# Seven block products for eight in the down projection of a hybrid decoder step

## The chip, the cores and the metric

The kernel runs on one core of one Trainium2 chip, in one launch. The core has a matrix engine (TensorE, PE in the profile), VectorE (DVE), ScalarE (ACT), GpSimd (POOL) and SyncE (SP), whose queue issues most transfers here. The metric is the time on the device in microseconds (us). Three runs of the kernel before took 1352.70, 1354.54 and 1359.77 us, median 1354.54.

## The reference, cut to what matters

A prompt of 1024 positions and 8 sample rows (1032 columns together) pass a layer: RMSNorm, a wide input projection, four groups of heads, an output projection with a residual add, and then the feed-forward part, which is what the change touches:

```
D_MODEL = 1024; D_FF = 2816; CONV_W = 3
def conv_ffn(x, g, w_up, conv_w, conv_b, w_down, buf):
    t = x.shape[1]
    up = rmsnorm(x, g) @ w_up
    ext = jnp.concatenate([buf.astype(up.dtype), up], axis=1)
    conv = conv_b + sum(ext[:, i:i + t] * conv_w[i] for i in range(CONV_W))
    a, gate = jnp.split(conv, 2, axis=-1)
    y = (jax.nn.silu(gate) * a) @ w_down
    return y, ext[:, t:]
...
        xp = xp + f.astype(xp.dtype)
```

The down projection is the product with `w_down` (2816 x 1024) and the residual add behind it. All is float32.

## The kernel before, in words

Everything is transposed: features lie on the 128 partitions, positions in the columns. A float32 product is made of three products of reduced-precision parts (`f32r`): each operand x is split into high = round(x) on ScalarE (an `ACTIVATE` with Copy) and low = x - high on VectorE (a `TENSOR_TENSOR`), and TensorE adds hi*hi + hi*lo + lo*hi in PSUM. So every tile of an operand costs one pass on ScalarE and one on VectorE before TensorE can take it.

The **up projection** runs over 22 pairs of tiles (`FT = 22`, index p or c). Each p is already seven block products P1 to P7 (a Strassen-Winograd scheme over half-blocks), each of 24 matmuls of 258 columns (`HC = 258`; two chunks make half of the 1032 columns, 516). Convolution, silu and the gate product follow on VectorE and ScalarE, and SP stores the resulting activation tile `va` to `scr_act[p]` in DRAM (`act_store`, L848).

The **down projection** before goes over eight output tiles d, 22 contraction tiles f and three column chunks of 344. Its activations are loaded back from `scr_act` (L864), split once, and kept in SBUF in all 22 tiles (`fh`, `fl`). The weights come in 24 groups (`GRAN`): a load (`down_load`, L857), a high split (`down_hi`, L1900), a low split (`down_low`, L2750), with two buffers in turn. The matmuls are L1410 to L1412. The first four groups serve d = 0 and 1 together; then one output tile after the other is finished, `add_y` (L2824) adds its PSUM banks to the residual loaded by GpSimd (L2938), and GpSimd stores it (L2933). Tiles d alternate between two sets of three banks, so the next tile's matmuls go on while one is evicted. The last tile is finished by chunk (L2835) and stored by SP (L900).

What sets the order is the code alone: each engine runs its own list, written out by hand, and waits on counting semaphores. `p_done` counts finished products or groups of TensorE (`NPROD` of them before the down projection), `st_hi` and `st_lo` the weight splits, `mv_hi` and `mv_lo` the activation splits, `x2_add` the evictions, `act_st` the stores of activations. An engine that waits holds all that stands behind it in its list; SP's list of loads too.

Of the kernel before, what the change touches and what calls it, by code (L numbers as in the profile page):

```python
# [18 lines left out]
P = 128  # L19
# [12 lines left out]
CH = 344  # L32
# [66 lines left out]
def build(nc, t):  # L99
# [5 lines left out]
    with ctx:  # L105
# [161 lines left out]
        fh = []  # L267
        for n, o5 in ((0, Q), (1, Q + 8256), (2, set0), (3, set0 + 8256), (4, Q + 16512), (5, Q + 24768), (6, Q + 33024),
                      (7, Q + 41280), (12, set1), (13, set1 + 8256), (14, set1 + 16512), (19, conv0), (20, conv0 + 8256),
                      (21, base)):  # L270
            h_, o6 = at(f"fh{n}", [P, COLS], f32r, o5)
            fh.append((n, h_[:, :], at(f"fl{n}", [P, COLS], f32r, o6)[0][:, :], at(f"fr{n}", [P, COLS], f32, o6)[0][:, :]))
        fh = {n: (h_, l_, r_) for n, h_, l_, r_ in fh}
        for j in range(KC):
            fh[8 + j if j < 4 else 11 + j] = (hhi[:, j, :], hlo[:, j, :], hlr[:, j, :])
        dst2 = [spare, set0 + 16512]
        dnh, dnl, dnr = [], [], []
        for n in range(2):
            h_, o6 = at(f"dnh{n}", [P, 1024], f32r, dst2[n])
            dnh.append(h_)  # L280
            dnl.append(at(f"dnl{n}", [P, 1024], f32r, o6)[0])
            dnr.append(at(f"dnr{n}", [P, 1024], f32, o6)[0])
        yst = at("yst", [P, COLS], f32, base + 8256)[0]
# [191 lines left out]
        NG = len(GRAN)  # L475
        g_end = {d: max(n for n in range(NG) if d in GRAN[n][0]) for d in range(KC)}
# [81 lines left out]
        def _(sp):  # L558
# [291 lines left out]
            def down_load(n):  # L850
                dd, fa_, fb_ = GRAN[n]
                w = len(dd) * P
                if n >= 2:
                    sp.wait_ge(S("p_done"), NPROD + n - 1)
                src = dnL[fa_:fb_, :, dd[0] * P:dd[0] * P + w].rearrange("f p c -> p f c")
                dst = dnr[n % 2][:, 0:(fb_ - fa_) * w].rearrange("p (f c) -> p f c", c=w)
                sp.dma_start(dst, src).then_inc(S(f"wgt_ld{n % 2}"), 16)  # L857
            def act_loads(done, p, fs):
                sp.wait_ge(S("p_done"), p_no[done, p])
                for f in fs:  # L860
                    sp.wait_ge(S("act_st"), 16 * (f + 1))
                    if f >= 4:
                        sp.wait_ge(S(f"stage_ld{f % 4}"), 16 * (12 + f // 4))
                    sp.dma_start(fh[f][2], scr_act[f]).then_inc(S(f"stage_ld{f % 4}"), 16)  # L864
            for c in range(FT):
# [23 lines left out]
            sp.wait_ge(S("act_st"), 16 * FT)
            act_loads("P3", FT - 1, (19, 20))  # L890
# [6 lines left out]
            for ch in range(3):
                sp.wait_ge(S("x2_add"), 2 * KC + ch)
                cs = slice(ch * CH, (ch + 1) * CH)
                sp.dma_start(t["o_yT"][:, KC - 1, cs], yst[:, cs]).then_inc(S("out"), 16)  # L900
            sp.wait_ge(S("out"), 16 * (3 + 3))
            sp.wait_ge(S("y_out"), 16 * (KC - 1))
# [51 lines left out]
        def _(pe):  # L954
# [446 lines left out]
            def down(n, d, f, chs, first, last):  # L1401

                dd, fa_, fb_ = GRAN[n]
                w = len(dd) * P
                c = (f - fa_) * w + (d - dd[0]) * P
                hi_, lo_ = dnh[n % 2][:, c:c + P], dnl[n % 2][:, c:c + P]
                a_hi, a_lo, _ = fh[f]
                for ch in chs:
                    out, cs = ps[:, 3 * (d % 2) + ch, 0:CH], slice(ch * CH, (ch + 1) * CH)
# [26 lines left out]
        def _(act):  # L1436
# [465 lines left out]
            for c in range(FT):  # L1902
                more = c + 1 < FT
                if c:
# [11 lines left out]
                    if more:  # L1916
                        w_vec(c + 1)
# [1082 lines left out]
```

## Time and profile before

| | |
|---|---|
| Median of the runs shown | 1354.54 us (1352.70 to 1359.77) |
| Profiled execution: span | 1348.4 us |
| Its own time beside the span | not recorded; the median of the runs is 6.1 us more than its span |
| TensorE busy | 1302.1 us, 97% of the span |
| VectorE, ScalarE, GpSimd busy | 946.2, 555.1 and 217.1 us |
| Moved by DMA | 206.82 MB, mean 153 GB/s |
| Down projection, first matmul to the end | 1092.79 to 1345.4 us |

The page gives busy time by engine, then the chain of work that ended last, followed back from the last instruction. Matmuls overlap: each shows about 0.28 or 0.32 us of its own while one starts every 0.12 or 0.16 us, so the pace is read from starts, and a wait from the idle time in square brackets. Between 700 and 1060 us the profile is periodic (18 pairs p); from 1132 us on it is periodic by output tile.

### The profile page before, as it was taken

To read this page: it belongs to the slowest core of one execution; us is meant where nothing else is said; L and a number is where in the kernel's file an instruction comes from. 1 tells how busy PE (TensorE), PEld (TensorE's weight loads), DVE (VectorE), ACT (ScalarE), POOL (GpSimd) and SP (SyncE) were. 2 spreads that over 40 slices of the span, in tenths; PEclk is the share of its full clock that TensorE was granted. 3 is DMA by queue.
4 is the path that set the end of the run, shared out by engine and by line. 5 is a ranking of instruction groups with operands and counts; after the bars stand their busy time and mean duration, and the time that the engine had idled before them with its cause. 6 is when DMAs were issued, how large, how long until landed. Compare 5 with 4: busy or idle time off the path is not lost.

```text
span 1348.4 us, 24281 instructions
## 1 busy us (share of the span) xinstructions
PE 1302.1 (97%) x9271; PEld 1198.1 (89%) x9271; DVE 946.2 (70%) x1390; ACT 555.1 (41%) x913; POOL 217.1 (16%) x222
## 2 busy tenths in 40 slices
PE   7999999989989999999999999999999999999999
PEld 5888787767667678899999999999999998999999
DVE  6678889988898767567697888887788894211111
ACT  6623111355567665343545435445445463000100
POOL 0420034323333430100201101101101000000000
PEclk9999999979999999999999999999999999999999
DMA  9868766679999772421322222222222383322222
GB/s 304 302 208 252 208 176 182 211 225 259 295 322 354 227 224 76 148 97 62 94 88 70 96 71 71 95 71 71 96 71 71 124 302 115 106 85 81 75 75 75
DMA packets 151071, 206.82 MB, mean 153 GB/s; under 512 B 12862, under 2 KB 112728, under 8 KB 150676
## 3 DMA queue, kind: packets, MB, share of 16 engines
q1 hardware_dynamic: 133204, 146.74, 35.0%
q0 software_dynamic: 12848, 46.73, 10.9%
q10 hardware_dynamic: 4904, 11.81, 2.9%
q8 instruction: 73, 1.20, 0.4%
q14 instruction: 42, 0.34, 0.1%
HBM read 174.91 MB, written 29.82 MB: 152 GB/s over the span
## 4 chain that ended last, share of the span: by engine, by line
PE 74%; DVE 10%; DMA 5%; issue 3%; POOL 3%; SPq 3%; ACT 1%; ACTq 0%; DVEq 0%; POOLq 0%
PE ps L1349 9%; PE ps L1350 9%; PE ps L1351 9%; PE ps L1410 6%; PE ps L1411 6%; PE ps L1412 6%; PE ps L1191 4%; PE ps L1132 3%; PE ps L1134 3%; PE ps L1133 3%; PE ps L1214 2%; PE ps L1290 1%; DMA upr<-in_w_upL 1%; PE ps L1292 1%; PE ps L1291 1%
## 5 line engine op out<-in xcount | busy, mean ns | idle before, releaser
L1349 PE MATMUL ps<-hhi,uph 128*128 128x258 f32 x704 | 200.8, 285 | 1.3 <-ACT ug L1828 0.7
L1350 PE MATMUL ps<-hlo,uph 128*128 128x258 f32 x704 | 199.5, 283 | 0.0
L1351 PE MATMUL ps<-hhi,upl 128*128 128x258 f32 x704 | 199.2, 283 | 0.0
L2750 DVE TENSOR_TENSOR dnl<-dnr,dnh 128x896 fp32r<-128x896 f32 (+2 forms) x24 | 27.2, 1135 | 176.3 <-ACT dnh L1900 176.3
L1349 PEld LDWEIGHTS ps<-hhi,uph 128*128 128x128 f32 x704 | 133.9, 190 | 2.6 <-DVE ug L2708 1.4
L1350 PEld LDWEIGHTS ps<-hlo,uph 128*128 128x128 f32 x704 | 134.1, 190 | 0.0
L1351 PEld LDWEIGHTS ps<-hhi,upl 128*128 128x128 f32 x704 | 133.6, 190 | 0.0
L1132 PE MATMUL ps<-whi,hhi 128*128 128x512 f32 (+1 forms) x336 | 125.7, 374 | 0.9 <-PE ps L1134 0.6
L1134 PE MATMUL ps<-whi,hlo 128*128 128x512 f32 (+1 forms) x336 | 124.4, 370 | 0.0
L1133 PE MATMUL ps<-wlo,hhi 128*128 128x512 f32 (+1 forms) x336 | 124.0, 369 | 0.0
L1410 PE MATMUL ps<-fh,dnh 128*128 128x344 f32 x336 | 107.5, 320 | 3.2 <-DVE dnl L2750 3.2
L1411 PE MATMUL ps<-fl,dnh 128*128 128x344 f32 x336 | 107.8, 321 | 0.0
L1412 PE MATMUL ps<-fh,dnl 128*128 128x344 f32 x336 | 107.2, 319 | 0.0
L1900 ACT ACTIVATE dnh<-dnr 128x896 fp32r<-128x896 f32 (+2 forms) x24 | 23.7, 987 | 194.7 <-DMA dnr<-in_w_down 194.7
L2925 POOL TENSOR_TENSOR upr<-upr 128x512 f32<-128x512 f32 x22 | 30.8, 1398 | 447.0 <-DMA upr<-in_w_upL 447.0
L1191 PEld LDWEIGHTS ps<-vst,pts 128*128 128x128 f32 x576 | 72.3, 198 | 30.4 <-issue 27.4
L1769 ACT ACTIVATE uph<-upr 128x1024 fp32r<-128x1024 f32 (+1 forms) x66 | 79.3, 1202 | 39.6 <-DMA upr<-in_w_upL 36.1
L2628 DVE TENSOR_TENSOR upl<-upr,uph 128x1024 fp32r<-128x1024 f32 (+1 forms) x66 | 92.1, 1396 | 0.1
L1191 PE MATMUL ps<-vst,pts 128*128 128x65 f32 x576 | 79.5, 285 | 9.1 <-DVE oN L2333 7.1
L2862 POOL DMA_INDIRECT vring<-in_cache_a_v,gtab x64 | 62.3, 973 | 137.0 <-PE ps L1214 130.8
L2020 DVE TENSOR_TENSOR ring<-ring,qb 128x1024 f32<-128x1024 f32 x64 | 78.0, 1218 | 7.3 <-DMA ring<-in_cache_a_k 5.7
L2028 DVE TENSOR_REDUCE sA<-ring 128x16 f32<-128x1024 f32 x64 | 78.0, 1219 | 1.9
(357 smaller groups left out, 3567.2 us busy)
## 6 DMA issues: line engine op xcount, KB each, us to landing
upr<-in_w_upL SPq DMA_DIRECT2D x88, 256.0 KB, 3.3
ring<-in_cache_a_k SPq DMA_DIRECT2D x170, 128.0 KB
scr_act<-va SPq DMA_DIRECT2D x22, 516.0 KB, 2.6
ring<-in_cache_a_k ACTq DMA_DIRECT2D x86, 128.0 KB
wst<-in_w_in SPq DMA_DIRECT2D x32, 256.0 KB, 3.9
fr<-scr_act SPq DMA_DIRECT2D x14, 516.0 KB, 5.2
dnr<-in_w_down SPq DMA_DIRECT2D x12, 448.0 KB, 4.2
dnr<-in_w_down SPq DMA_DIRECT2D x10, 512.0 KB, 4.0
```

The source lines that it names most:

```text
L1132: pe.matmul(out, lh, whi[:, sl, 0:w], start=(kc == 0), stop=False)
L1133: pe.matmul(out, lh, wlo[:, sl, 0:w], start=False, stop=False)
L1134: i = pe.matmul(out, ll, whi[:, sl, 0:w], start=False, stop=(kc == KC - 1))
L1191: i = pe.matmul(ps[:, 6, 0:HD + 1], pts[:, g % 2, j, :], vst[:, hp % 2, j, VCOL[H % 2]], start=(j == 0), stop=(j == nb - 1))
L1349: pe.matmul(out, hi_, r_hi[:, cs], start=(first and i == 0), stop=False, skip_group_check=not first)
L1350: pe.matmul(out, hi_, r_lo[:, cs], start=False, stop=False, skip_group_check=not first)
L1351: m = pe.matmul(out, lo_, r_hi[:, cs], start=False, stop=(i == 3), skip_group_check=not first)
L1410: pe.matmul(out, hi_, a_hi[:, cs], start=first, stop=False)
L1411: pe.matmul(out, hi_, a_lo[:, cs], start=False, stop=False)
L1412: m = pe.matmul(out, lo_, a_hi[:, cs], start=False, stop=last)
L1769: act.activation(uph[p % 2][:, a:b, :], upr[p % 2][:, a:b, :], ACT.Copy).then_inc(S("st_hi"), 1)
L2628: dve.tensor_tensor(upl[p % 2][:, a:b, :], upr[p % 2][:, a:b, :], uph[p % 2][:, a:b, :].bitcast(f32), ALU.subtract).then_inc(S("st_lo"), 1)
```

## The change

The down projection becomes a Strassen-Winograd scheme too. The output has two halves by feature (mi: 4 tiles each) and two by position (ni: 516 columns each), the contraction two halves of 11 tiles (`HK = 11`). With A the weight, B the activations, blocks A11 to A22 and B11 to B22:

- S3 = A11 - A21, S2 = A21 + A22 - A11, S1 = A21 + A22, S4 = A12 - S2; T3 = B22 - B12, T2 = B11 + T3, T4 = B21 - T2, T1 = B22 - T2 (the names are the code's; S2 and T4 stand there with a sign)
- P1 = A11 B11, P2 = A12 B21, P6 = S2 T2, P7 = S3 T3, P4 = A22 T4, P5 = S1 T1, P3 = S4 B22
- in PSUM: P1, then P2 on top of it gives output block 11; P6 alone, P7 on top, P4 on top; P5 alone, P3 on top. P1 is copied to SBUF (`u_p1`) before P2 goes on top, and added to three quarters of the residual by GpSimd.

The order of products is `PHASE`, 11 steps each, 77 steps in all (`NSTEP`). A step is one contraction tile: 516 columns of activations, 512 of weights, four output tiles by two chunks by three terms, 24 matmuls of 258 columns, over all eight banks. So a product fills all banks, and the next one may write bank pair j only when it is copied or evicted (`bank_free`). Operands are no longer split once and kept: every step splits its own into a ring of four slots (`bh`, `bl`, `wh`, `wl`; raw weights in `wr`), a slot is free when TensorE has finished the step four before. Raw activations stay in SBUF (`act_t`) and GpSimd forms the T sums in place; VectorE forms the S sums (`w_sum`), GpSimd S1. Weights are loaded as single tiles of 256 KB by `ring_load`, `wa_load` and `wb_load`; the residual comes in four quarters of 1.06 MB (`x_quarter`), and SP stores the output (`y_store`).

```diff
-        GRAN = [((0, 1), f, f + 4) for f in (0, 4, 8, 12)] + [((d,), 16, FT) for d in (0, 1)] \
-            + [((d,), a, b) for d in range(2, KC) for a, b in ((0, 8), (8, 15), (15, FT))]
+        PHASE = ["P1", "P2", "P6", "P7", "P4", "P5", "P3"]
+        NSTEP = len(PHASE) * HK
...
+            def ring_load(st):
...
+                sp.wait_ge(S("p_done"), NPROD + st - 3)
+                sp.dma_start(wr[st % 4][:, :], down_w(mi, HK + k)).then_inc(S(f"ring_ld{n % 4}"), 16)
...
+            for st in range(HK, NSTEP):
+                ph, k = PHASE[st // HK], st % HK
+                if st in RING_NO:
+                    ring_load(st)
+                if ph == "P2":
+                    if k == 1:
+                        x_quarter(1, xq1, 0, 1)
+                    if k == 3:
+                        x_quarter(2, xq2, 1, 1)
+                    wb_load(k)
+                if st == step_of("P6", 3):
+                    for j in range(4):
+                        y_store("P2", j)
+                if st == step_of("P6", 6):
+                    sp.wait_ge(S("y_out"), 16 * 4)
+                    x_quarter(3, xq0, 1, 0)
...
+            def bank_free(ph, j):
+                if ph == "P1":
+                    pe.wait_ge(S("c_sum"), 5 * (FT - 1) + (-1, 1, 3, 4)[j])
+                    return
+                if ph == "P2":
+                    pe.wait_ge(S("copied"), 3 * FT + j + 1)
+                    return
+                pe.wait_ge(S("x2_add"), KC + 4 * (PHASE.index(ph) - 2) + j + 1)
+            for st in range(NSTEP):
+                ph, k = PHASE[st // HK], st % HK
+                n = st % 4
+                pe.wait_ge(S("mv_lo"), MV0 + st + 1)
+                pe.wait_ge(S("st_lo"), ST0 + st + 1)
+                fresh = ph in FRESH
+                for j in range(4):
+                    if k == 0:
+                        bank_free(ph, j)
+                    hi_, lo_ = wh[n][:, j * P:(j + 1) * P], wl[n][:, j * P:(j + 1) * P]
+                    for ch in range(2):
+                        out, cs = ps[:, 2 * bank_of[j] + ch, 0:HC], slice(ch * HC, (ch + 1) * HC)
+                        pe.matmul(out, hi_, bh[n][:, cs], start=(fresh and k == 0), stop=False, skip_group_check=not fresh)
+                        pe.matmul(out, hi_, bl[n][:, cs], start=False, stop=False, skip_group_check=not fresh)
+                        m = pe.matmul(out, lo_, bh[n][:, cs], start=False, stop=(k == HK - 1), skip_group_check=not fresh)
...
+            for st in range(4, NSTEP):
+                b_hi(st)
+                w_hi(st)
+                if st == HK + 2:
+                    for j in range(4):
+                        p1_copy(j)
...
+            for st in range(4, NSTEP):
+                if st + 1 < NSTEP and PHASE[(st + 1) // HK] != "P2":
+                    w_sum(st + 1)
+                b_lo(st)
+                w_lo(st)
+                if PHASE[st // HK] == "P2":
+                    w_sum(st)
+                ph = PHASE[(st - 3) // HK]
+                if (st - 3) % HK == HK - 1 and ph in EVICT:
+                    for j in range(4):
+                        evict(ph, j)
...
+            for k in range(HK):
+                n = RING_NO[step_of("P4", k)]
+                pool.wait_ge(S(f"ring_ld{n % 4}"), ring_total(n))
+                pool.wait_ge(S("s_vec"), VEC_NO["S3", k])
+                summed(w_b[k][:, :], w_b[k][:, :], wr[step_of("P4", k) % 4][:, :], ALU.add)
```

`w_sum` waits for `ring_ld` of its step in P6, P4 and P3 and does nothing for P7 and P5; in P2 it forms S3 behind the splits. `b_hi(st)` waits until step st - 4 is finished, `evict` for its bank pair (`pair_done`, or `p_done` for the last).

Three places of the new order follow. First VectorE, where P2 ends and P6 begins: step 24 is the third of P6 (its slot is `wr_208`), `wr_213` is step 25's raw weight, `xq_225` the quarter of the residual that takes P2's banks.

```order
L2914 TENSOR_TENSOR wr_208<-wr_208,wa_185 128x512 [waits s_vec,ring_ld0]
L2894 TENSOR_TENSOR bl_221<-act_162,bh_220 128x516 [waits mv_hi]
L2902 TENSOR_TENSOR wl_224<-wr_223,wh_222 128x512 [waits st_hi]
L2914 TENSOR_TENSOR wr_213<-wr_213,wa_186 128x512 [waits s_vec,ring_ld1]
L2894 TENSOR_TENSOR bl_206<-act_163,bh_205 128x516 [waits mv_hi]
L2902 TENSOR_TENSOR wl_209<-wr_208,wh_207 128x512 [waits st_hi]
L2943 TENSOR_TENSOR xq_225<-ps,xq_225 128x516 [waits y_ld,pair_done]
L2943 TENSOR_TENSOR xq_225<-ps,xq_225 128x516 [waits pair_done] x2
L2943 TENSOR_TENSOR xq_225<-ps,xq_225 128x516 [waits p_done]
```

The four evictions of P2 (L2943) stand behind step 25's weight sum and the splits of step 24. In the kernel before, an eviction was one instruction of 1032 columns behind a weight split, and TensorE was by then on the other set of banks:

```order
L2750 TENSOR_TENSOR dnl_204<-dnr_205,dnh_203 128x1024 [waits st_hi]
L2824 TENSOR_TENSOR yst<-ps,yst 128x1032 [waits y_ld,p_done]
L2750 TENSOR_TENSOR dnl_207<-dnr_208,dnh_206 128x896 [waits st_hi]
L2824 TENSOR_TENSOR yst<-ps,yst 128x1032 [waits y_ld,p_done]
L2750 TENSOR_TENSOR dnl_204<-dnr_205,dnh_203 128x896 [waits st_hi]
```

ScalarE, where P1 ends and P2 begins: `wr_213` is step 13's weight, `u_p_228` the copy of P1.

```order
L2043 ACTIVATE wh_222<-wr_223 128x512 [waits ring_ld3]
L2032 ACTIVATE bh_205<-act_173 128x516 [waits stage_ld0,p_done]
L2043 ACTIVATE wh_207<-wr_208 128x512 [waits ring_ld0]
L2032 ACTIVATE bh_210<-act_174 128x516 [waits stage_ld1,p_done]
L2043 ACTIVATE wh_212<-wr_213 128x512 [waits ring_ld1]
L2048 ACTIVATE u_p_228<-ps 128x516 [waits pair_done] x3
L2048 ACTIVATE u_p_228<-ps 128x516 [waits p_done]
```

The copies stand behind the high split of a weight that has to be loaded first. SP's list at the same place, from the last two halves of activations on (`act_171`, `act_182`); `wr_213` is again step 13's weight:

```order
L934 DMA act_171<-scr_act 128x516 [waits x_ld0]
L934 DMA act_182<-scr_act 128x516 [waits act_st,x_ld1]
L954 DMA wr_223<-in_w_down 128x512 [waits p_done]
L947 DMA wb_194<-in_w_down 128x512
L954 DMA wr_208<-in_w_down 128x512 [waits p_done]
L959 DMA xq_226<-scr_x 128x4x516 [waits y_ld]
L947 DMA wb_195<-in_w_down 128x512
L954 DMA wr_213<-in_w_down 128x512 [waits p_done]
```

The ring's first weight loads stand behind all 40 loads of activations; between them stand two loads of A21 and one quarter of the residual. In the kernel before, all weight loads from the fifth on had SP to themselves.

## Rows read from the trace of the kernel before

**Rows 1.** The page: busy time by engine, and the chain that ended last.

```profile
PE 1302.1 (97%) x9271; PEld 1198.1 (89%) x9271; DVE 946.2 (70%) x1390; ACT 555.1 (41%) x913; POOL 217.1 (16%) x222
...
PE 74%; DVE 10%; DMA 5%; issue 3%; POOL 3%; SPq 3%; ACT 1%; ACTq 0%; DVEq 0%; POOLq 0%
```

**Rows 2.** Windows: busy us (instructions) by engine, granted clock, DMA share, GB/s.

```profile
700.00:1060.00 360.00, 359.37 (x2981) 358.43 (x2981) 295.29 (x320) 159.98 (x231) 46.99 (x36) 1.00 0.25 80
...
1132.00:1340.00 208.00, 208.00 (x1325) 208.00 (x1324) 38.18 (x35) 23.90 (x25) 7.48 (x14) 1.00 0.26 80
```

**Rows 3.** Timeline at the seams: start, us, engine, line, shapes, [idle before].

```profile
1092.79 0.32 PE L1410 MATMUL ps<-fh,dnh 128*128 128x344 f32 x1
...
1126.63 0.32 PE L1412 MATMUL ps<-hhi,dnl 128*128 128x344 f32 x1
1130.19 0.43 PE L1410 MATMUL ps<-fh,dnh 128*128 128x344 f32 x1 [3.24 <-DVE dnl L2750]
...
1345.26 0.32 PE L1412 MATMUL ps<-fh,dnl 128*128 128x344 f32 x1
...
1345.62 0.52 DVE L2835 TENSOR_TENSOR yst<-ps,yst 128x344 f32<-128x344 f32 x1 [2.78 <-PE ps L1412]
```

**Rows 4.** The chain that ended last, around the 3.24 us gap.

```profile
1128.91 1.24 DVE dnl L2750
1130.15 0.04 issue
```

**Rows 5.** Windows where the clock fell, rose and stayed; timeline at one fall.

```profile
278.00:279.00 1.00, 0.65 (x5) 0.68 (x6) 0.97 (x2) 0.98 (x2) 0.73 (x1) 0.87 1.07 369
...
285.00:286.00 1.00, 1.00 (x7) 0.85 (x6) 0.69 (x1) 0.28 (x1) 0.00 (x0) 0.71 1.18 310
...
288.00:289.00 1.00, 0.48 (x5) 0.51 (x5) 0.93 (x6) 0.00 (x0) 0.00 (x0) 0.99 0.44 143
...
295.00:296.00 1.00, 1.00 (x9) 0.83 (x12) 0.91 (x3) 0.22 (x2) 0.00 (x0) 0.59 0.42 139
...
456.00:457.00 1.00, 1.00 (x5) 0.98 (x6) 0.69 (x4) 0.80 (x4) 0.08 (x1) 0.62 0.89 274
...
459.00:460.00 1.00, 1.00 (x16) 0.17 (x8) 0.83 (x2) 0.13 (x1) 0.17 (x1) 0.68 0.56 229
...
534.00:535.00 1.00, 0.00 (x0) 0.00 (x0) 0.96 (x3) 0.61 (x3) 0.02 (x1) 0.87 0.00 0
...
541.00:542.00 1.00, 1.00 (x8) 1.00 (x8) 1.00 (x1) 0.00 (x0) 0.00 (x0) 0.72 1.02 405
...
1128.00:1129.00 1.00, 0.00 (x0) 0.00 (x0) 0.09 (x1) 1.00 (x2) 0.00 (x0) 1.00 0.71 179
...
535.63 0.55 PE L1300 MATMUL ps<-hhi,wohi 128*128 128x256 f32 x1 [2.25 <-DVE hlo L2440]
```

**Rows 6.** Landing of 256 KB loads: L568 (2 KB rows), then L813 (512 B).

```profile
DMA to landing us min/median/max: 2.0/3.9/8.2
...
DMA to landing us min/median/max: 2.9/3.1/4.4
```

**Rows 7.** Timeline: an eviction-like DVE pass, a copy, a GpSimd sum.

```profile
1086.26 0.60 ACT L1828 ACTIVATE ug<-ps 128x516 f32<-128x516 f32 x1 [4.24 <-PE ps L1351]
...
1087.28 0.69 DVE L2708 TENSOR_TENSOR ug<-ps,ug 128x516 f32<-128x516 f32 x1
1088.00 0.69 DVE L2714 SCALAR_TENSOR_TENSOR ug<-ug,rstd_bc 128x516 f32<-128x516 f32 x1
...
1056.96 1.31 POOL L2925 TENSOR_TENSOR upr<-upr 128x512 f32<-128x512 f32 x1 [18.24 <-DMA upr<-in_w_upL]
```

**Rows 8.** SP's last activation store; then windows around the seam.

```profile
1105.81 0.38 SPq L848 DMA_DIRECT2D scr_act<-va  x1
...
1090.00:1100.00 10.00, 10.00 (x71) 10.00 (x70) 8.72 (x11) 6.84 (x11) 0.00 (x0) 1.00 1.00 388
1100.00:1110.00 10.00, 10.00 (x66) 10.00 (x65) 9.96 (x10) 6.08 (x7) 0.00 (x0) 1.00 0.80 272
```

More of the change, by code:

```diff
@@ L273, in build @@
[L273 to L283, printed above, removed]
+        HK = FT // 2
@@ new lines, in build @@
+        RING_NO = {}
+        for ph_ in ("P1", "P2", "P6", "P4", "P3"):
+            for k_ in range(HK):
+                RING_NO[step_of(ph_, k_)] = len(RING_NO)
+        POOL_NO = {}
+        for name_ in ("T3", "T2"):
+            for k_ in range(HK):
+                POOL_NO[name_, k_] = 2 * FT + 2 * k_ + (1 if name_ == "T3" else 2)
+        for name_ in ("x12", "x22"):
+            POOL_NO[name_] = 2 * FT + 2 * HK + (1 if name_ == "x12" else 2)
+        for k_ in range(HK):
+            POOL_NO["T4", k_] = POOL_NO["x22"] + k_ + 1
@@ L858, in act_loads, with act_load @@
[L858 to L864, printed above, removed]
+            def act_load(f, full=False):
+                sp.wait_ge(S("act_st"), 16 * (f + 1))
+                if f >= 4:
+                    sp.wait_ge(S(f"stage_ld{f % 4}"), act_total(f - 4))
+                c = slice(0, COLS if full else H2)
+                sp.dma_start(act_t[f][:, c], scr_act[f, :, c]).then_inc(S(f"stage_ld{f % 4}"), 16)
@@ new lines, in _ @@
+                    for f in range(4):
+                        act_load(f, True)
+                    sp.wait_ge(S("p_done"), p_no["P5", FT - 1])
+                    for k in range(8):
+                        wa_load(k)
+            sp.wait_ge(S("p_done"), p_no["P2", FT - 1])
+            for f in range(4, 8):
+                act_load(f)
+            sp.wait_ge(S("p_done"), p_no["P7", FT - 1])
+            for f in range(8, 16):
+                act_load(f)
+            sp.wait_ge(S("p_done"), p_no["P3", FT - 1])
@@ L897, in _ @@
[L897 to L902, printed above, removed]
+            for f in H2_ORDER[0:8]:
+                act_load2(f)
+            sp.wait_ge(S("act_st"), 16 * FT)
+            act_load(21)
+            for f in H2_ORDER[8:]:
+                act_load2(f)
@@ L1399, in _ @@
                 seven("P3", p, slotY[p], S4_, B22, False)
[L1401 to L1409, printed above, removed]
-                    pe.matmul(out, hi_, a_hi[:, cs], start=first, stop=False)
-                    pe.matmul(out, hi_, a_lo[:, cs], start=False, stop=False)
-                    m = pe.matmul(out, lo_, a_hi[:, cs], start=False, stop=last)
-                return m
@@ L1917, in _ @@
                         w_vec(c + 1)
+                    else:
+                        w_hi(0)
+                        w_hi(1)
                     silu(c - 1)
+                    if not more:
+                        b_hi(2)
+                        w_hi(2)
                     u3_copy(c)
```

361 lines of the change are left out of this document (236 added, 125 removed).

## The prediction, made before the changed kernel ran

> **What bounds the kernel now.** I read the page first. TensorE is busy for 97% of the span and carries 74% of the chain that ended last [rows 1]. The change touches the down projection alone, so the second view is two stretches of steady matmuls, one of the up projection (258 columns) and one of the down projection (344) [rows 2]: in both TensorE is never idle for more than a fraction of a microsecond, VectorE is 82% busy in the first and 18% in the second. The third is TensorE's timeline at the seams [rows 3]: the down projection starts at 1092.79, loses one gap of 3.24 us at 1126.95, and its last matmul starts at 1345.26. So the stage is 252.6 us of TensorE, bound by the array's own pace, and everything else hides behind it. After it come one eviction of 0.52 us and one store.
>
> **The work.** Before: 8 output tiles x 22 contraction tiles x 3 column chunks x 3 terms = 1584 matmuls. The first 216 (three groups of 72) take 34.0 us up to the gap, 0.1574 us each; all of them are 249.3 us, and 252.6 - 249.3 = 3.3 us is the gap. After: 77 steps x 4 output tiles x 2 chunks x 3 terms = 1848 matmuls of 258 columns. That shape runs before the seam: 2981 in 360 us, 0.1208 us each [rows 2], so 223.2 us, and 2.90 us for one step of 24. The block products alone give -26.1 us, one eighth of the columns back and a fixed piece per matmul lost on 264 more matmuls. The old gap waited for a weight load that stood behind a store and an output on SP; that order goes, -3.3. Without any wait of its own the new stage is 29.4 us shorter.
>
> **What feeds it.** The operands are no longer split once and kept: each step splits 516 activation columns and 512 weight columns on ScalarE (0.6 each, as the copy) and VectorE (0.69 each, as the two evictions) [rows 7], at most 2.1 us of VectorE per step with a weight sum, against 2.90. GpSimd's 22+11+11 sums of 516 columns and 11 of 512 take 1.3 us each [rows 7], three adds of 2064 columns perhaps 5.2 each: 88 us over 223. T3 and T2 are wanted a whole product later. None of these is the bound by its sum. What counts is order, in three kinds of place.
>
> **a) The eviction behind the next load (P2 to P6, P7 to P4, P5 to P3).** A weight slot is refilled when the step four before is finished. VectorE's row has, ahead of the four evictions of a product, the weight sum of the *next* step, whose load SP asks for only when the product's last step is finished (the order rows of the change). TensorE's next product may not write a bank until it is evicted. So at the product's end everything runs in line: tail of the last matmul and wake-up 0.2 (a 344-column matmul lasts 0.32 at a pace of 0.157; 0.04 from VectorE's end to TensorE's start [rows 4]), landing of 256 KB, wake-up 0.1, then sum, two splits and the first eviction, 4 x 0.67 = 2.7 us. Lone loads of 256 KB landed in 3.1 us (median, pieces of 512 B) and the fastest one with 2 KB rows in 2.0 [rows 6]; I take the middle, 2.6. Gap: 0.2 + 2.6 + 0.1 + 2.7 = 5.6 us, bounds 5.0 and 6.1. Three: +16.8 us (15.0 to 18.3). The later evictions cost 0.69 against 0.72 us of matmuls per tile, so only the first is paid. Where P7 follows P6 and P5 follows P4 no load stands ahead; the splits end some 2.0 us after a step, the eviction 0.7 later, still inside a step.
>
> On that landing the Trainium skill ("DMA: Bandwidth & Descriptors", section "Anatomy of one DMA") gives 2.0 us fixed and the bytes at 436 GB/s: an estimate of 2.6 us for 256 KB, inside the two rows. That fit is for transfers issued by GpSimd; no row here shows a lone SP load with 2 KB rows.
>
> **b) P1 to P2.** ScalarE copies P1's banks out behind the high split of step 13's weight. SP reaches that load late. Its last store of activations was asked for at 1105.8 [rows 8]; VectorE now does less ahead of it, so about 1103. Behind it stand u10 (0.4 MB), 18 second halves and one first (5.0 MB), with the store 5.9 MB. At 330 GB/s, between 272 and 388 of the rows [rows 8], that is 18 us; the first weight load of the ring is asked for near 1120. Ahead of step 13's load lie then 0.8 MB of halves, four weight tiles (1.0 MB) and a quarter of x2 (1.06 MB): with its own 0.26, 3.2 MB, 9.6 us, so it lands near 1129.3. Split and first copy, 1.2: P2 starts at 1130.5. P1 ends at 1092.8 + 11 x 2.90 = 1124.7. Gap: 5.8; I take 5.5 us, 2.5 at 388 GB/s, 10 at 272.
>
> **c) The ring inside P6, P4 and P3.** A step's splits stand behind the next step's sum, so they end 0.2 + landing + 0.1 + 3 x 0.67 after the step three before; they are due two steps (5.8 us) after it. With 2.6 that is 4.9: 0.9 us to spare. It holds, but a 1 MB quarter and twice four stores pass in P6 to P5: +0.5.
>
> **d) The clock.** The granted clock fell from 2.4 to 1.2 GHz four times before the up projection [rows 5]. From the levels, the low stretches are 278.74-285.58, 288.98-295.82, 456.24-459.64 and 534.74-541.56, the last with TensorE idle until 535.63. Half of the busy time in them is lost: 3.4, 3.4, 1.7 and 3.0, mean 2.9 us. The last followed 2.25 us of idleness [rows 5], among the attention's short matmuls. Against that stands one 3.24 us gap between full-length matmuls, after which the clock was still whole (1128-1129). The new gaps are 5 to 6 us, so nearer to full idleness than any of them. I count the three of a) as falling: +8.7, bounds 0 and 4 x 3.4 = 13.6.
>
> The Trainium skill ("TensorE: Matmul & The Clock Gate", section "HAM oscillation — how this bites in real kernels") tells of a kernel that waits for a transfer at each tile and starts each next tile at the low clock. By that rule all four gaps fall, +11.6 instead of +8.7; by the 3.24 us row none need to. The four falls side with the page.
>
> **Sum.** -29.4 + 16.8 + 5.5 + 0.5 + 8.7 = +2.1 us. The profiled span is 1348.4 us; it has no own time beside it, the median of the runs shown is 1354.5, 6.1 more, which I leave as it is. Forecast 1356.6 us. Its bounds: -29.4 + 15.0 + 2.5 = -11.9 (1342.6) to -29.4 + 18.3 + 10 + 4.4 + 13.6 = +16.9 (1371.4), where 4.4 is the price of the slow ring below.
>
> **Rivals.**
> *The clock stays.* Full-length matmuls before and after each gap, as at 1127: the sum without d), -6.6 us, 1347.9. For it that one row, against it that the new gap is nearly twice as long.
> *No gaps: the change does what its work says.* The ring's load is early enough, or evictions overlap: -29.4 and some 2 for the seams, 1327. Against it is VectorE's order, which is fixed.
> *Transfers bind (slower).* The place is the ring in P6, P4, P3; it decides from a landing of 3.5 us on, where 0.2 + L + 0.1 + 2.0 passes 5.8. With all queues loaded the 256 KB loads had a median of 3.9 [rows 6]. Then a step takes (6.2 + 2.9)/3 = 3.03 us, 33 x 0.13 = +4.4; each gap a) is 1.3 longer, +3.9; b) is 10, +4.5: 1356.6 + 12.8 = 1369.4. For it: 1 MB quarters and stores on the same queue. Against it: a step moves 0.26 MB in 2.90 us, 90 GB/s, and the queues did 388.
>
> **Chances.** Forecast 0.48, spread 1350 to 1363; clock stays 0.17; no gaps 0.07; transfers bind 0.28. About 0.5% (6.8 us) is what a measurement of this kernel tells from no change: faster means under 1347.8, slower over 1361.3. Faster: all of the second rival, half of the first (0.09), 0.03 of the forecast, 0.19. Slower: most of the third (0.22) and 0.07 of the forecast, 0.29. Same 0.52. Range: from a clock that stays with quick landings, 1344, to the third rival, 1369.
>
> **What will show it.** TensorE with 1848 matmuls at 0.121 us and four idle spells: the first ended by ScalarE's copy, the other three by VectorE's eviction, each 5 to 6 us, with the weight load issued right at the product's end. The granted clock near 0.5 for 3 to 7 us behind them. No gap at P6 to P7 and P4 to P5 above 0.5 us. Waits at single steps inside P6, P4 or P3 would speak for the third rival. I am wrong if the three gaps are absent or under 3 us, if the copy of P1 comes in time, or if matmuls of 258 columns run slower with this operand pattern than in the up projection.

## The result

The changed kernel took 1388.47 us (median of 4 runs, 1386.09 to 1389.79) against 1353.62 us of the kernel before beside it (4 runs, 1347.31 to 1359.77): ratio 1.0257, 95% interval 1.0218 to 1.0296. It is 2.6% slower; 1356.6 us was forecast, and the forecast's range ended at 1369.

The two profiled executions have spans of 1348.4 and 1386.2 us, +37.8. First the page of the changed kernel, beside [rows 1]: busy time by engine, and the chain that ended last.

```profile
PE 1287.6 (93%) x9535; PEld 1180.7 (85%) x9535; DVE 1083.3 (78%) x1557; ACT 601.3 (43%) x1025; POOL 310.0 (22%) x265
...
PE 53%; DVE 20%; DMA 11%; SPq 6%; issue 5%; POOL 3%; ACT 2%; ACTq 0%; another core or an unknown queue 0%; DVEq 0%; POOLq 0%
```

TensorE is busy for 14.5 us less than before and the span is longer: the work did shrink, and waits took more than its place. TensorE's share of the chain fell from 74% to 53%, and VectorE and the transfers have what it lost. Stretches of the down projection, for comparison with [rows 2] (columns as there):

```profile
1095.00:1127.00 32.00, 31.51 (x265) 31.30 (x263) 22.26 (x25) 11.88 (x21) 10.66 (x8) 1.00 0.93 307
1127.00:1159.00 32.00, 14.03 (x96) 13.85 (x96) 25.89 (x12) 10.67 (x19) 31.00 (x17) 0.78 0.69 226
1159.00:1184.00 25.00, 20.41 (x151) 19.90 (x152) 25.00 (x22) 4.22 (x7) 18.83 (x12) 0.88 0.31 85
1304.00:1350.00 46.00, 40.88 (x338) 40.62 (x339) 26.82 (x44) 16.31 (x28) 0.00 (x0) 0.99 0.14 47
```

Read the VectorE column (the third pair) against the number of instructions in brackets: 44 passes in 26.8 us in the last row, but 12 passes in 25.9 us and 22 in 25.0 in the two rows where GpSimd (the fifth pair) is busy for most of the stretch. The waits of TensorE, to be set beside [rows 3] with its single gap of 3.24 us:

```profile
1139.38 0.55 PE L1556 MATMUL ps<-bh,wh 128*128 128x258 f32 x1 [12.87 <-ACT u_p L2048]
...
1161.76 0.55 PE L1556 MATMUL ps<-bh,wh 128*128 128x258 f32 x1 [8.35 <-DVE wl L2902]
...
1191.51 0.55 PE L1556 MATMUL ps<-bh,wh 128*128 128x258 f32 x1 [5.27 <-DVE xq L2943]
...
1216.79 0.55 PE L1556 MATMUL ps<-bh,wh 128*128 128x258 f32 x1 [5.96 <-DVE wl L2902]
...
1226.99 0.36 PE L1556 MATMUL ps<-bh,wh 128*128 128x258 f32 x1 [2.00 <-DVE wl L2902]
...
1276.01 0.55 PE L1556 MATMUL ps<-bh,wh 128*128 128x258 f32 x1 [6.44 <-DVE xq L2943]
...
1349.48 0.55 PE L1556 MATMUL ps<-bh,wh 128*128 128x258 f32 x1 [5.12 <-DVE xq L2943]
```

With six more of 0.42 to 1.68 us there are 13 gaps, 51.85 us. Three are the evictions of a), 16.83 us; one is b), 12.87; nine, 22.15 us, were not forecast. The granted clock was at 1.2 GHz behind six of the 13 and costs 12.2 us (busy time times the missing part of the clock, summed over windows of 1 us: 2.63 behind b), 2.18, 2.60 and 1.58 behind the three of a), 1.69 and 1.48 behind the gaps of 8.35 and 5.96). The account: matmuls -26.1, gaps 51.85 - 3.24 = +48.6, clock +12.2, the stage starts 2.1 us later (1094.90 for 1092.79; in the runs below it starts anywhere from 1087 to 1101, so 2.1 is no more than scatter of the part before it): +36.8 of the 37.8.

**What VectorE does beside GpSimd.** VectorE around the gap of 8.35 us:

```profile
1148.17 1.79 DVE L2902 TENSOR_TENSOR wl<-wr,wh 128x512 fp32r<-128x512 f32 x1
1149.88 5.11 DVE L2910 TENSOR_TENSOR wa<-wa,wb 128x512 f32<-128x512 f32 x1
1154.92 5.02 DVE L2894 TENSOR_TENSOR bl<-act,bh 128x516 fp32r<-128x516 f32 x1
1159.86 1.75 DVE L2902 TENSOR_TENSOR wl<-wr,wh 128x512 fp32r<-128x512 f32 x1
```

and GpSimd in the same microseconds:

```profile
1147.84 1.57 POOL L3110 TENSOR_TENSOR act<-act 128x516 f32<-128x516 f32 x1
1149.38 10.01 POOL L3110 TENSOR_TENSOR xq<-xq,u_p 128x2064 f32<-128x2064 f32 x2
```

The same VectorE instruction that takes 0.69 us alone [rows 7] takes 1.75 to 1.80 us (two passes fall outside this, 1.56 and 1.84) beside GpSimd sums of 512 or 516 columns, and 4.6 to 5.1 us beside adds of 2064. In these rows the two engines alternate: one VectorE pass for each GpSimd instruction, whatever its length. Held up is the instruction that starts second. The 19 other VectorE passes of the stage that overlap a GpSimd sum began before it; they took 0.68 to 0.69 us, and it is mostly GpSimd's sum that became longer:

```profile
1170.06 0.68 DVE L2902 TENSOR_TENSOR wl<-wr,wh 128x512 fp32r<-128x512 f32 x1
...
1170.22 1.68 POOL L3110 TENSOR_TENSOR act<-act,act 128x516 f32<-128x516 f32 x1 [0.63 <-DVE bl L2894]
```

In P2 a step has three passes of the slow kind, 3 x 1.70 (start to start) = 5.10 us, against 2.90 us of matmuls. The Trainium skill ("SBUF — State Buffer", section "Who interferes with whom") says that a VectorE instruction with two inputs in SBUF contends with a GpSimd instruction that reads SBUF. The trace agrees, with 0.69 us against 1.77 and 5.0.

Another reading would be that GpSimd's sums come late to those who need them. The trace speaks against it: between 1095 and 1385 us no wait of TensorE, VectorE or ScalarE is ended by GpSimd, and it is VectorE's passes themselves that are long. The run with the sums on VectorE, below, needs every sum in full and has none of these waits.

**The gap of 12.87 us.** SP's list at the end of P1 (P1's last matmul started at 1126.23):

```profile
1107.37 11.00 SPq L934 DMA_DIRECT2D act<-scr_act  x8
1118.48 0.37 SPq L924 DMA_DIRECT2D act<-scr_act  x1
1119.58 8.04 SPq L934 DMA_DIRECT2D act<-scr_act  x10
1127.66 0.43 SPq L954 DMA_DIRECT2D wr<-in_w_down  x1
...
1130.11 0.70 SPq L954 DMA_DIRECT2D wr<-in_w_down  x1
```

and ScalarE, whose copy of P1's banks releases TensorE:

```profile
1132.45 0.63 ACT L2043 ACTIVATE wh<-wr 128x512 fp32r<-128x512 f32 x1 [13.84 <-DMA wr<-in_w_down]
...
1138.12 0.63 ACT L2043 ACTIVATE wh<-wr 128x512 fp32r<-128x512 f32 x1 [2.92 <-DMA wr<-in_w_down]
1138.66 2.06 ACT L2048 ACTIVATE u_p<-ps 128x516 f32<-128x516 f32 x4
```

The ring's first load is asked for at 1127.66, after P1's end; step 13's, asked for at 1130.11, has landed by 1138.12 and the copy stands behind its split. (The 11.00 and 8.04 us of the first rows run from the first to the last of several requests.)

**One gap of a), at P5 to P3.** VectorE:

```profile
1346.83 0.69 DVE L2921 TENSOR_TENSOR wr<-wr,wa 128x512 f32<-128x512 f32 x1 [0.21 <-DMA wr<-in_w_down]
...
1348.64 2.49 DVE L2943 TENSOR_TENSOR xq<-ps,xq 128x516 f32<-128x516 f32 x4
```

SP asks for the load at 1344.38, as the product ends; 2.45 us to the sum, 1.81 us for three passes, 0.84 from the first eviction's start to TensorE's at 1349.48: 5.1 us.

### The profile page after: what moved, and what is told of

Its sections match the earlier page's. It is cut to its first block, busy times and chain, and to the rows that moved or that the text cites. A ratio compares the mean times of both kernels' runs of the same rounds, so it can differ in the third digit from the quotient of the medians.

```text
span 1386.2 us, 25416 instructions
## 1 busy us (share of the span) xinstructions
PE 1287.6 (93%) x9535; PEld 1180.7 (85%) x9535; DVE 1083.3 (78%) x1557; ACT 601.3 (43%) x1025; POOL 310.0 (22%) x265
## 4 chain that ended last, share of the span: by engine, by line
PE 53%; DVE 20%; DMA 11%; SPq 6%; issue 5%; POOL 3%; ACT 2%; ACTq 0%; another core or an unknown queue 0%; DVEq 0%; POOLq 0%
PE ps L1480 7%; PE ps L1481 7%; PE ps L1482 7%; PE ps L1322 4%; PE ps L1556 4%; PE ps L1558 3%; PE ps L1557 3%; DMA act<-scr_act 2%; DMA upr<-in_w_upL 2%; DVE bl L2894 2%; DVE wl L2902 2%; PE ps L1345 2%; PE ps L1303 2%; SPq L431 1%; DMA ring<-in_cache_c_k 1%
## 5 line engine op out<-in xcount | busy, mean ns | idle before, releaser
L1556 PE MATMUL ps<-bh,wh 128*128 128x258 f32 x616 | 181.7, 295 | 52.2 <-DVE wl L2902 20.5
L1557 PE MATMUL ps<-bl,wh 128*128 128x258 f32 x616 | 178.5, 290 | 0.0
L1558 PE MATMUL ps<-bh,wl 128*128 128x258 f32 x616 | 177.5, 288 | 0.0
L1556 PEld LDWEIGHTS ps<-bh,wh 128*128 128x128 f32 x616 | 121.3, 197 | 55.1 <-issue 53.9
L1558 PEld LDWEIGHTS ps<-bh,wl 128*128 128x128 f32 x616 | 122.1, 198 | 0.0
L1557 PEld LDWEIGHTS ps<-bl,wh 128*128 128x128 f32 x616 | 122.0, 198 | 0.0
L2894 DVE TENSOR_TENSOR bl<-act,bh 128x516 fp32r<-128x516 f32 x77 | 78.2, 1016 | 22.3 <-ACT bh L2032 22.3
```

What stands on the lines that cost most here:

```text
L1556: pe.matmul(out, hi_, bh[n][:, cs], start=(fresh and k == 0), stop=False, skip_group_check=not fresh)
L1557: pe.matmul(out, hi_, bl[n][:, cs], start=False, stop=False, skip_group_check=not fresh)
L1558: m = pe.matmul(out, lo_, bh[n][:, cs], start=False, stop=(k == HK - 1), skip_group_check=not fresh)
L2894: dve.tensor_tensor(bl[st % 4][:, :], operand(st), bh[st % 4][:, :].bitcast(f32), ALU.subtract).then_inc(S("mv_lo"), 1)
```

## The experiments

Gaps and clock are those of the profiled execution between 1090 and 1390 us (gaps from 0.4 us on); the ratio is to the kernel before. Variants with GpSimd's sums of 8 columns, with its copies, and with the gaps filled don't compute the layer's result; they are there for the time alone.

| kernel | median us | ratio (95%) | gaps us | clock us |
|---|---|---|---|---|
| changed kernel | 1388.5 | 1.026 (1.022 to 1.030) | 51.9 | 12.2 |
| evictions after the splits | 1377.8 | 1.017 (1.011 to 1.022) | 43.6 | 14.6 |
| GpSimd's adds in pieces | 1386.4 | 1.027 (1.021 to 1.033) | 50.5 | 17.1 |
| early ring loads | 1392.7 | 1.029 (1.023 to 1.035) | 47.9 | 18.0 |
| GpSimd's sums of 8 columns | 1360.0 | 1.005 (1.002 to 1.007) | 31.2 | 8.8 |
| the same, evictions one step earlier | 1337.7 | 0.987 (0.983 to 0.991) | 15.5 | 2.5 |
| sums on VectorE | 1373.4 | 1.012 (1.008 to 1.015) | 38.2 | 11.5 |
| sums on VectorE, early ring | 1361.9 | 1.007 (1.005 to 1.010) | 27.5 | 10.4 |
| sums on VectorE, evictions earlier | 1341.5 | 0.991 (0.988 to 0.995) | 16.7 | 2.5 |
| changed kernel, gaps filled | 1385.1 | 1.024 (1.019 to 1.029) | 34.9 | 8.0 |
| GpSimd copies for sums | 1363.4 (one run) | | 32.4 | 9.0 |
| all three | 1324.9 | 0.976 (0.973 to 0.980) | 5.6 | 1.5 |

### GpSimd's sums of 8 columns

```diff
-                pool.tensor_tensor(out, a, b, op).then_inc(S("s_sum"), 1)
+                if len(out.shape) == 3:
+                    out, a, b = out[:, 0, :], a[:, 0, :], b[:, 0, :]
+                pool.tensor_tensor(out[:, 0:8], a[:, 0:8], b[:, 0:8], op).then_inc(S("s_sum"), 1)
```

> Leaves out of the computation all but 8 columns of each of GpSimd's 58 sums in the down projection; their order and semaphores stay. Theory A (GpSimd's sums slow VectorE's passes): every pass of 512 or 516 columns is back at 0.69 us, the nine waits of together 22.2 us go and 4 us of clock with them, the three gaps of 5 to 6 us stay: 1362 us (1357 to 1368). Rival B (the waits come from late transfers, the slow passes do not matter): no more than 5 us go.

Measured 1360.0 us. The nine waits are gone to the last; the three of a) are 5.26, 5.16 and 5.22 us and the one of b) is 15.57. The lines of one group between 1095 and 1385 us, first in the changed kernel, then here:

```profile
L2910 DVE TENSOR_TENSOR wa<-wa,wb 128x512 f32<-128x512 f32 x11 | 22.9, 2080 | 0.0
```

```profile
L2910 DVE TENSOR_TENSOR wa<-wa,wb 128x512 f32<-128x512 f32 x11 | 7.6, 691 | 2.4 <-DMA wb<-in_w_down 2.4
```

The same eleven passes, 2080 ns and 691 ns. All of VectorE in that stretch: 205.5 and 144.3 us, so a GpSimd sum cost VectorE 61.2 / 58 = 1.06 us. Rival B, late transfers, falls: the loads are as they were, and 28.5 us went where it allowed 5.

### GpSimd's adds in pieces

```diff
-                summed(buf[:, :, :], buf[:, :, :], u_p1[:, :, :], ALU.add)
+                for j in range(3):
+                    pool.tensor_tensor(buf[:, j, :], buf[:, j, :], u_p1[:, j, :], ALU.add)
+                summed(buf[:, 3, :], buf[:, 3, :], u_p1[:, 3, :], ALU.add)
...
-            summed(xq0[:, :, :], xq0[:, :, :], u_p1[:, :, :], ALU.add)
+            for j in range(3):
+                pool.tensor_tensor(xq0[:, j, :], xq0[:, j, :], u_p1[:, j, :], ALU.add)
+            summed(xq0[:, 3, :], xq0[:, 3, :], u_p1[:, 3, :], ALU.add)
```

> GpSimd's three adds of 2064 columns are cut in four of 516 columns each; nothing else is changed. Theory A (a VectorE pass with two operands in SBUF has to wait for the end of the GpSimd instruction that runs beside it): VectorE's passes of 4.6 to 5.1 us near 1150, 1155 and 1209 come down to 1.8 us, the gaps of 8.35 and 5.96 us shrink by 3 to 6 us each and one fall of the clock less: 1379 us (1374 to 1384). Rival B (what is lost is a share of bandwidth, the same whatever the length of the instruction): VectorE still gets through the same number of passes in these 10 us, and the time stays within 2 us of 1388.5.

Neither theory came out whole. The passes did become short, as A has it, so VectorE waits for one GpSimd instruction at a time; from 1149.4 to 1159.6 us it now does six passes, where it did two between 1149.9 and 1159.9, so B's "same number of passes" is wrong:

```profile
1149.37 1.78 DVE L2910 TENSOR_TENSOR wa<-wa,wb 128x512 f32<-128x512 f32 x1
1151.07 1.79 DVE L2894 TENSOR_TENSOR bl<-act,bh 128x516 fp32r<-128x516 f32 x1
1152.79 1.76 DVE L2902 TENSOR_TENSOR wl<-wr,wh 128x512 fp32r<-128x512 f32 x1
```

But the time, 1386.4, cannot be told from 1388.5; it is 2.4 past the end of A's range (and 0.1 past B's 2 us). VectorE's slow pace is now TensorE's:

```profile
1154.69 0.36 PE L1556 MATMUL ps<-bh,wh 128*128 128x258 f32 x1 [1.99 <-DVE wl L2902]
...
1159.80 0.36 PE L1556 MATMUL ps<-bh,wh 128*128 128x258 f32 x1 [2.00 <-DVE wl L2902]
```

These starts are 5.11 us apart, three VectorE passes of 1.70. The gap of 8.35 us became several of 2 us, 18 us in eleven places for 22.2 in nine, while the copy's gap came out longer (15.8) and the clock's loss went from 12.2 to 17.1 us. So A is right on the mechanism and wrong on what it is worth: the length of a GpSimd instruction decides how a wait is dealt out. That the waits add up to nearly the same either way is what this run shows; why P1 to P2 and the clock took back what the waits gave was not pursued.

### Evictions after the splits

```diff
-                if st + 1 < NSTEP and PHASE[(st + 1) // HK] != "P2":
-                    w_sum(st + 1)
                 b_lo(st)
                 w_lo(st)
...
                     for j in range(4):
                         evict(ph, j)
+                if st + 1 < NSTEP and PHASE[(st + 1) // HK] != "P2":
+                    w_sum(st + 1)
```

> Only VectorE's order is changed: the two splits of a step, then the four evictions of a finished product, and the next step's weight sum last. Theory A (the three gaps of 5.27, 6.44 and 5.12 us that an eviction ends are evictions queued behind a load that is asked for at the product's end): these three fall under 2 us, 16.8 us and half of the clock's 12.7 us go, 1366 us (1360 to 1372). Rival B (VectorE is short of time there as such, because its passes take 1.77 instead of 0.69 us beside GpSimd): the gaps come back as waits for a split, and the time stays over 1380.

A miss for both: 1377.8 lies between A's range and B's 1380. The gaps are 5.19, 3.79 and 2.69 us, not under 2 as A has it, and the time they gave did not come back as waits for a split, as B has it. VectorE ahead of the second of them shows the reasons, and GpSimd's row beside it:

```profile
1272.29 1.75 DVE L2917 TENSOR_TENSOR wa<-wr,wa 128x512 f32<-128x512 f32 x1
1273.97 0.68 DVE L2894 TENSOR_TENSOR bl<-act,bh 128x516 fp32r<-128x516 f32 x1
1274.58 0.68 DVE L2902 TENSOR_TENSOR wl<-wr,wh 128x512 fp32r<-128x512 f32 x1
1275.18 2.49 DVE L2943 TENSOR_TENSOR xq<-ps,xq 128x516 f32<-128x516 f32 x4
...
1274.82 1.56 POOL L3110 TENSOR_TENSOR wb<-wb,wr 128x512 f32<-128x512 f32 x1 [1.32 <-DMA wr<-in_w_down]
```

One weight sum and two splits, of the third step of the next product, are still ahead of the evictions, and the sum runs at GpSimd's pace. The evictions don't: the first two, which read one operand from PSUM, begin while a GpSimd sum is under way and still take 0.68 us each. The next run moves the evictions ahead of these too, with the contention taken away.

### The same sums of 8 columns, evictions one step earlier

```diff
-                ph = PHASE[(st - 3) // HK]
-                if (st - 3) % HK == HK - 1 and ph in EVICT:
+                ph = PHASE[(st - 2) // HK]
+                if (st - 2) % HK == HK - 1 and ph in EVICT:
```

This on top of the order above and of the sums of 8 columns.

> As the run with GpSimd's sums of 8 columns (the same computation left out), and VectorE evicts a finished product one step earlier in its row: ahead of the weight sum of the step that needs the product's own freed slot. Theory A (in the first reordering VectorE still had one late load, that of the third step of the next product, ahead of the evictions, and GpSimd's contention in one of the three places): all three gaps of 5.2 us fall under 1 us and their falls of the clock go, 15 + 4 to 5 us: 1341 us (1337 to 1346). Rival B (the gap is the eviction and the splits themselves, whatever their order): the gaps stay over 3 us, the time over 1350.

1337.7 us, 22.3 less than with the same sums and the old order; 19 were expected. No gap but the one of b) is above 0.4 us, and the clock's loss falls from 8.8 to 2.5 us. The gaps of a) are an order of instructions.

### Early ring loads and copy

```diff
             for f in H2_ORDER[0:8]:
                 act_load2(f)
+            ring_load(HK)
+            wb_load(0)
...
                 b_hi(st)
-                w_hi(st)
                 if st == HK + 2:
                     for j in range(4):
                         p1_copy(j)
+                w_hi(st)
```

> SP asks for the weight tiles of P2's first four steps between the second halves instead of behind them, two quarters of x2 three steps later, and ScalarE copies P1's banks ahead of step 13's high split. Theory A (the gap of 12.87 us is the late weight tiles and the copy behind them): the gap falls under 4 us, with its fall of the clock 9 to 12 us go, 1378 us. Rival B (in P2 VectorE has three passes of 1.77 us beside GpSimd for a step of 2.90 us, so what the copy wins is waited out at the next steps): the gap at the copy goes, waits of the same sum appear in P2, the time stays within 4 us of 1388.5.

1392.7 us: A's gap came (12.87 down to 3.54) but not its time; the time is nearer to B's, 4.2 us from 1388.5 where B allowed 4. The loads and the copy were moved together, so their shares of the gap are not told apart. P2 then waits for splits at the pace of three slow passes, and the gap of 8.35 us is there again with 8.53; the clock's loss went from 12.2 to 18.0 us.

### The sums on VectorE

```diff
-            def summed(out, a, b, op):
-                pool.tensor_tensor(out, a, b, op).then_inc(S("s_sum"), 1)
+            def sum_of(name, k):
+                def summed(out, a, b, op):
+                    dve.tensor_tensor(out, a, b, op).then_inc(S("s_sum"), 1)
...
+                for name, k in SUM_AT.get(st, []):
+                    sum_of(name, k)
```

`SUM_AT` lists the sums of a step: T3 and T2 from step 9 to 28, T4 and eight pieces of the residual adds in P7, S1 in P4, T1 and the last four pieces from P4's end to P5's.

> All of GpSimd's sums of the down projection run on VectorE, the 44 sums of activations and 11 of weights as passes of 512 or 516 columns, the three adds of 2064 as twelve of 516, spread so that no step has more than four or five passes; SP's and ScalarE's order and the place of the evictions stay. Theory A (one such pass costs VectorE 0.6 us of its own, but 1.1 us where GpSimd does it beside another pass): VectorE is busy for fewer us in the stage though it does 67 passes more, the nine waits of 22.2 us go, the three gaps of 5 us stay: 1364 us (1358 to 1372). Rival B (VectorE has no room for 67 passes more: P2 has four of them per step of 2.90 us, and they wait for second halves): waits for splits stay in P2 and P6, the time over 1378.

1373.4 us, 9 above the middle of A and 1.4 past the end of its range; B's 1378 was not reached either. The waits for splits inside the products are gone, VectorE is busy for 187.1 us in the stretch from 1095 to 1385 against 205.5, with 67 passes more in its list. What was missed: VectorE's fuller row puts the gaps that evictions end at 6.62, 1.57, 5.72, 4.45 and 5.14 us, 23.5 for the 16.8 of a) and 1.7 more, two of them where P7 and P5 start.

### Two of three, and all three

The same edits together; where the evictions come earlier, the sums that VectorE has taken over stand behind them.

> The sums on VectorE and the evictions ahead of the late weight sum; SP's and ScalarE's order stay as in the changed kernel. Theory A (order at the product's end costs the 23.5 us of gaps ended by an eviction in the run with the sums on VectorE, and 6 us of clock): 1373.4 - 29 = 1344 us (1339 to 1350), only the gap of 14 us at P1 to P2 stays. Rival B (the win of the three together hangs on the early ring loads): over 1355.

1341.5 us, as A has it: what is left is the gap at P1 to P2, 14.87, and two of 0.46 and 0.71.

> The sums on VectorE and the ring's first loads and P1's copy earlier; the evictions stay where the changed kernel has them. Theory A (with VectorE free in P2 the early loads now bring what they did not bring beside GpSimd's sums, 14 us of gap down to 3 and 3 us of clock): 1373.4 - 14 = 1359 us (1354 to 1365), the gaps at product ends stay. Rival B (VectorE, now with four passes a step in P2, eats it up as it did beside GpSimd): over 1368.

1361.9 us, as A has it: the copy's gap is 4.33 us, those at the products' ends stay. The loads that brought nothing beside GpSimd's sums bring 11.5 us here, from 1373.4.

> The sums on VectorE, the evictions ahead of the late weight sum, and the ring's first loads and P1's copy earlier, together. Theory A (contention, order and late ring loads are the three causes, and each hid part of the others): gaps a) and the nine waits under 3 us in all, the gap at P1 to P2 about 3.5 us, the clock's loss under 3 us: 1388.5 - 22 - 16 - 9 - 9 = 1332 us (1327 to 1342), faster than the kernel before by 1 to 2%. Rival B (what is left shows as waits for VectorE, which now carries everything): over 1350.

1324.9 us, 2.4% faster than the kernel before and 4.6% than the changed one. That is 7 us under A's 1332 and 2 below its range: the causes together gave more than was expected of them. Two stretches of P2 to P7, and the two longest gaps that are left:

```profile
1125.00:1160.00 35.00, 33.12 (x265) 32.97 (x265) 28.26 (x47) 14.40 (x26) 0.00 (x0) 0.95 0.75 258
...
1192.00:1224.00 32.00, 31.59 (x265) 31.41 (x265) 28.44 (x48) 13.06 (x23) 0.00 (x0) 1.00 0.08 26
```

```profile
1125.34 0.55 PE L1576 MATMUL ps<-bh,wh 128*128 128x258 f32 x1 [2.87 <-ACT u_p L2068]
...
1159.96 0.36 PE L1576 MATMUL ps<-bh,wh 128*128 128x258 f32 x1 [1.54 <-DVE xq L3005]
```

VectorE does 47 or 48 passes in a stretch like the one in which it did 12 beside GpSimd, and TensorE is busy again from end to end.

### The gaps filled

```diff
+                if k == 0 and ph in ("P6", "P4", "P3"):
+                    for i in range(40):
+                        m = pe.matmul(ps[:, 2 * bank_of[3] + i % 2, HC:512], wh[n][:, 0:P], bh[n][:, 0:512 - HC],
+                                      start=True, stop=True, skip_group_check=True)
+                    m.then_inc(S("fill"), 1)
```

VectorE's fourth eviction there waits for `fill`. The added matmuls write columns beside the fourth output tile's sums in its two banks.

> The changed kernel, with 40 matmuls of 254 columns more (4.8 us, their output is not used) ahead of the wait for the first eviction at P2 to P6, P7 to P4 and P5 to P3. Theory A (the clock falls because TensorE idles in these gaps): the gaps are as long as before but filled, their three falls of the granted clock go (1189 to 1196, 1274 to 1282, 1349 to 1353, together 7.5 us at 1.2 GHz): 4 to 6 us less, 1383 us (1379 to 1386). Rival B (the clock's falls are not tied to these gaps): the falls stay, 1388 us or more.

1385.1 us, 3.4 less, inside A's range; but the four runs of either kernel overlap, so the time alone decides nothing. The rows of the clock do. The windows at the first, second and third place:

```profile
1190.00:1195.00 5.00, 4.59 (x39) 4.42 (x38) 4.61 (x7) 3.36 (x6) 0.44 (x1) 1.00 0.33 105
...
1275.00:1280.00 5.00, 4.04 (x35) 3.83 (x33) 5.00 (x7) 0.63 (x1) 1.55 (x2) 1.00 0.15 50
1345.00:1350.00 5.00, 4.55 (x39) 4.35 (x37) 4.06 (x8) 1.79 (x3) 0.00 (x0) 1.00 0.19 56
```

The granted clock is whole in all three, where it had been at 1.2 GHz for 6.8, 6.8 and 3.4 us (17.1 in all, not the 7.5 of the expectation) and cost 6.4 us; in the whole stage it now costs 8.0 us instead of 12.2. At these three places TensorE's idleness is what brings the clock down.

### GpSimd copies in place of sums

```diff
-                pool.tensor_tensor(out, a, b, op).then_inc(S("s_sum"), 1)
+                pool.tensor_copy(out, a).then_inc(S("s_sum"), 1)
```

> GpSimd's 58 sums of the down projection become copies of one operand of the same size (so the sums are left out of the computation): one operand read instead of two. Theory A (VectorE's passes are slow beside any GpSimd instruction that reads and writes SBUF): still 1.3 us or more beside a copy. Rival B (they are slow only where GpSimd too reads two operands): 0.69 us, and the time is that of the run with sums of 8 columns, 1360.

1363.4 us in one run, and between the two theories. VectorE beside two copies of 2064 columns, then beside copies of 516:

```profile
1144.35 2.39 DVE L2902 TENSOR_TENSOR wl<-wr,wh 128x512 fp32r<-128x512 f32 x1
1146.67 1.10 DVE L2910 TENSOR_TENSOR wa<-wa,wb 128x512 f32<-128x512 f32 x1
```

One operand read by GpSimd is enough to hold VectorE up (B falls), but a copy of 516 columns takes GpSimd 0.61 us alone where a sum takes 1.3, so VectorE waits for less: 1.10 us a pass, not A's 1.3 or more.

## Why the prediction was wrong, step by step

- **The work, -29.4.** Right: the count is 1848, and the stretch of P1 shows the pace (265 matmuls in 31.51 us of busy time, 0.119 each). The -3.3 for the old gap and -26.1 for the matmuls both came.
- **What feeds it.** This is the step that failed. It said "at most 2.1 us of VectorE per step with a weight sum, against 2.90" and took GpSimd's 88 us as spread beside it. Both numbers were read from rows in which the other engine was idle [rows 7]. Together they don't hold: a pass costs 1.70 us from start to start while GpSimd sums, a P2 step 5.10 us. The price, between the changed kernel and the one with sums of 8 columns, is 28.5 us. In the two profiled executions it is 27.8: nine waits of 22.2, 3.4 of clock, 1.2 of a) and 0.7 of the stage's start, less 2.7 by which b) happens to be shorter; 3.1 are not accounted for. The sign was there before the change, in rows of that trace that the prediction did not use. A VectorE instruction of 8 columns in the up projection takes 1.14 to 1.34 us in the seven places where it starts behind one of GpSimd's sums or within 0.02 us of it, and 0.23 us alone; first such a pair, then the same VectorE line with GpSimd idle:

```profile
1036.13 1.23 DVE L2730 SCALAR_TENSOR_TENSOR va<-ua,prm_a,sbase 128x8 f32<-128x8 f32 x1
...
1036.04 1.30 POOL L2925 TENSOR_TENSOR upr<-upr 128x512 f32<-128x512 f32 x1 [17.65 <-DMA upr<-in_w_upL]
...
1056.35 0.23 DVE L2730 SCALAR_TENSOR_TENSOR va<-ua,prm_a,sbase 128x8 f32<-128x8 f32 x1
```

- **a) Eviction behind the load, +16.8.** Right in place, releaser and sum: 5.27, 6.44 and 5.12 us, 16.83. Alone they are 5.26, 5.16 and 5.22, so 0.4 under the 5.6 of the forecast, with 2.45 us from the load's request to the sum for the 2.7 of landing and wake-up; that the total of 16.8 came out exact is luck, because contention made one of them 1.3 us longer. With the order changed they go.
- **b) P1 to P2, +5.5.** Right mechanism, mis-sized term: 12.87 us, and 14.1 to 15.9 in the eight other runs with that order; the bound was 10. The first ring load was asked for at 1127.66, not near 1120: SP's last store of activations came at 1106.39, not 1103, and from there it was 21.3 us, where 18 were reckoned; the stretch from 1095 to 1127 moved 307 GB/s, not 330. From the first ring load to step 13's landing it was 10.5 us, near the 9.6 of the forecast.
- **c) The ring, +0.5.** Right: with GpSimd's sums cut to 8 columns no wait inside P6, P4 or P3 is above 0.4 us. The waits in P6 and P4 that the forecast would have put down to the third rival, transfers that bind, are contention; a late split of VectorE is named as their releaser, and with the sums cut short they are gone while the loads are the same.
- **d) The clock, +8.7.** All three of a) fell, as forecast, for 6.4 us in all instead of 8.7. The clock fell at three further gaps that were not counted, b) among them, for 5.8: 12.2 us. With b) the four gaps of the forecast cost 9.0 us: the 8.7 came near by three falls at 2.9 us each, where there were four of 2.2 on the average.
- **"No gap at P6 to P7 and P4 to P5 above 0.5 us".** Wrong at P6 to P7, 1.68 us, behind slow passes; right with sums of 8 columns.

None of the three rivals was what happened, and the forecast's own terms with the measured sizes (a 16.8, b 12.9, their clock 9.0, start 2.1, work -29.4) would give +11.4, 1366 us, still inside the range. The 22.2 + 3.2 us of contention carried it out. The 6.1 us that the sum added for the median of the runs above the profiled span came out at 2.3 in the changed kernel (1388.5 and 1386.2).

## What to carry to other kernels

When work is laid on GpSimd beside VectorE, ask first whether VectorE's instructions there read two operands from SBUF: then a pass and a sum follow each other and don't overlap (one VectorE pass every 1.70 us here, for 0.61 alone; 1.06 us for each GpSimd sum), and the sum may be cheaper on VectorE itself, about 0.6 us. A row of a trace in which one of the two was idle says nothing on that; look for the same line with the other engine busy. Evictions, with one operand in PSUM, kept their 0.68 us beside a GpSimd sum. Put evictions ahead of whatever waits for a load that the product's own end releases, and take causes away together before dismissing one: the early loads brought nothing with contention and 11.5 us without.

## What was not expected of the hardware

- VectorE and GpSimd alternate instruction by instruction: 1.77 us for a VectorE pass of 0.69 beside GpSimd sums of 516 columns, 5.0 beside adds of 2064, 1.10 beside copies of 516. A pass that began before the sum kept its 0.68. GpSimd pays less: 1.54 to 1.81 us for 1.27 to 1.31.
- How long a gap is does not alone say whether the clock falls: it stayed after 3.24 us in the kernel before and after 2.69 us in the first reordering (1344.30), and fell with 3.25 us there (1219.52), with 2.87 us in the run of all three (1125.34) and, in the run with adds in pieces, with a gap of 2.06 us (1297.33) that has no other of 0.4 us or more within 27 us of it. What tells them apart stays open.
